# First attention of a two-layer encoder: the sample queries' scores, maxima and exponentials take later places in three queues

## The chip, the cores and the metric

The kernel runs on one core of a Trainium2 chip. The metric is the device time of one execution in microseconds (us). TensorE (PE) multiplies matrices, VectorE (DVE) and ScalarE (ACT) work on tiles, GpSimd (POOL) does small elementwise work, SyncE (SP) issues the DMAs. Each engine takes its own instructions in the order in which the program lists them; a wait on a semaphore holds everything behind it on that engine.

## The reference

Two request groups share the weights: a prompt of 1024 tokens with no history, and a sample of 32 tokens with 512 cached ones. There are two layers; the first is differential attention with a block-causal mask, the second stick-breaking attention. Each branch has a SiLU gate, an output projection and a second gated addition. Only the first attention is touched.

```python
def _diff_attn(h, pos, w_in, ...):
    q, k, v, g = jnp.split(h @ w_in, 4, axis=-1)
    q = _rope(q...); k = _rope(k...)
    k_all, v_all = with the cached keys and values ahead
    lam = exp(sum(lq1 * lk1)) - exp(sum(lq2 * lk2)) + lam_init
    def block(qb, qpb):                       # 128 queries
        s = einsum('bqhcd,bkhcd->bhcqk', qb, kf) * A_DH ** -0.5
        mask = k_chunk[None, :] <= (qpb // CHUNK)[:, None]
        pr = softmax(where(mask, s, NEG_INF), axis=-1)
        w = pr[:, :, 0] - lam * pr[:, :, 1]
        return einsum('bhqk,bkhe->bqhe', w, vf)
    o = _rmsnorm(sweep(block), sub_g) * (1.0 - lam_init)
    return (o * silu(g)) @ w_out, k, v
```

There are 8 heads of two components (c = 0, 1) with 64 features each; keys and queries of a head fill 128 partitions together.

## The kernel before

`diff_layer` computes the first attention, one group for each of the 8 heads. Groups 1 to 7 run in a loop (`more` is true: they also prepare the next group), the eighth stands behind it (`more` is false). In a group the work is laid out by hand in stages j = 2 to 13, and each engine's program has its own list of what it does in stage j. There are nine units u of queries: 0 to 7 are 128 prompt queries against (u + 1) * 128 keys, and unit 8 (`NT`) is the 32 sample queries against 544 keys. In the text of the prediction, scores(8) is the scores of unit 8, and so on.

A unit goes through these steps, each in the queue of one engine:

- PE `scores(u)` (stage u + 2): matmuls of queries and keys into the PSUM tile `la_sc`, each product in three passes of high and low parts. From u = 4 on it waits until both `probs(u - 1)` have read the tile.
- DVE `maxima(u)` (stage u + 3): the mask, and for both components the row maximum (L606) and its negative (L608).
- ACT `probs(u, c)` (stage u + 3): exponentials (L418) into `la_p`, with their sums.
- DVE `combine(u)` (stage u + 4): reciprocals and the difference of the two components (L615 to L621); the result is called weights(u) in the prediction.
- PE `turn_weights(u, g)` (L807): transposes of these weights, group g = 0 in stage u + 4, g = 1 in stage u + 5.
- ACT `move(u, g)` (L436, L432): the transposed weights to SBUF.
- PE `values(c)` (L831): weights by values, for queries of units 0 to 3 (c = 0, stage 8), of units 4 to 7 (c = 1, stage 12), and of the sample (c = 2, stage 13).

Between these stand other pieces of work. Stages 9, 10 and 11 hold the gate's three pieces (0, 1, 2): PE `gate_project` in an early part (5 of 8 rows of weights) and a late part, ACT `gate_raw`, then for the piece of the stage before DVE `gate_clamp`, ACT `gate_log`, DVE `gate_soft`, ACT `gate_sigmoid`, and POOL's product. In the same stages ACT (`split_w`, L390, tile `la_w_high`) and DVE (`split_w`, L569, tile `la_w_low`) split the next group's weight rows 0 to 2, 3 to 5 and 6 to 7 into high and low parts. From stage 12 on PE projects the first two token tiles of the next group (`project(ahead, ...)`, L105): the early part uses rows 0 to 4, the late part rows 5 to 7, and for the first tile it waits for each row's low part.

The order in stages 10 and 11 of the kernel before is:

| stage | PE | DVE | ACT |
|---|---|---|---|
| 10 | gate 1 early, turn_weights(5,1), gate 1 late, scores(8), turn_weights(6,0) | maxima(7), gate_clamp(0), combine(6), gate_soft(0), split rows 3 to 5 | probs(7), move(5,1), gate_log(0), gate_raw(1), gate_sigmoid(0), move(6,0), split rows 3 to 5 |
| 11 | gate 2 early, turn_weights(6,1), gate 2 late, turn_weights(7,0) | maxima(8), gate_clamp(1), combine(7), gate_soft(1), split rows 6, 7 | probs(8), move(6,1), gate_log(1), gate_raw(2), gate_sigmoid(1), move(7,0), split rows 6, 7 |

Stage 12 is: on PE the early part of the first tile ahead, turn_weights(7,1), its late part, turn_weights(8,0), values(1); on DVE gate_clamp(2), combine(8), gate_soft(2), finish(0); on ACT move(7,1), gate_log(2), gate_sigmoid(2), move(8,0).

Of the kernel before, what the change touches and what calls it, by code (L numbers as in the profile page):

```python
# [32 lines left out]
NT = SEQ // P  # L33
# [191 lines left out]
def diff_layer(nc, top, name, h, w_in, k_past, v_past, k_out, v_out, o_dram, w_out, ident, neg_lam, gain, cos, sin, stage):  # L225
# [14 lines left out]
    def groups_of(u):  # L240

        if u == NT:
            return [(0, PB + 1)]
        return [(k, min(4, u + 1 - k)) for k in range(0, u + 1, 4)]
# [4 lines left out]
    with ExitStack() as ctx:  # L249
# [19 lines left out]
                     scores=9, neg_max=18, probs=18, weights=9, w_turned=13, moved=13, pv=3, squared=3, var=3, log=3,  # L269
# [113 lines left out]
        def _(act):  # L383
# [19 lines left out]
            def turned_high(at, t):  # L403
                act.wait_ge(S["turned"], at.nth("turned", t + 1))
                act.activation(qk[0][:, :, tile_cols(t)], turned_bank(t), ACT.Copy).then_inc(S["turned_high"], 1)

            def body(r, more):
# [14 lines left out]
                def move(u, g):  # L422
                    q0, n, nk = UNITS[u]
                    if u < 4:
                        act.wait_ge(S["pv"], at.before("pv"))
                    elif u == 4:
                        act.wait_ge(S["pv"], at.nth("pv", 1))
                    act.wait_ge(S["w_turned"], at.nth("w_turned", moves_before(u) + g + 1))
                    k0, nb = groups_of(u)[g]
                    bank = pj[:, 2, 0:nb * n].rearrange("p (b n) -> p b n", n=n)  # L430
                    if u == NT:
                        act.activation(wt_sample[:, 0:PB, :], bank[:, 0:PB, :], ACT.Copy)  # L432
                        ins = act.activation(wt_sample[0:DEC, PB, :], bank[0:DEC, PB, :], ACT.Copy)
                    else:
                        off = q0 % QC
                        ins = act.activation(wt[:, k0:k0 + nb, off:off + n], bank, ACT.Copy)  # L436
                    ins.then_inc(S["moved"], 1)
# [35 lines left out]
                def next_tokens(t):  # L473

                    act.wait_ge(S["pv"], at.nth("pv", 2))
                    act.wait_ge(S["tok_stored"], at.all("tok_stored"))
                    tokens(ahead, t)

                for j in range(2, LAST + 1):
                    if more and j == 13:  # L480
                        next_tokens(0)
                    if j == 9:
                        square(0)
                    if j == LAST:
                        square(1)
                    if 0 <= j - 3 <= NT:
                        probs(j - 3, 0)
                        probs(j - 3, 1)
                    if j <= 9:
                        turned_high(at, j - 1)  # L490
                    if 0 <= j - 5 <= NT and len(groups_of(j - 5)) > 1:
                        move(j - 5, 1)
                    if j - 1 in GATE_AT:
                        gate_log(GATE_AT[j - 1])
                    if j <= 8:
                        act.wait_ge(S["pv"], at.before("pv"))
                        tokens(at, j)
                    if j in GATE_AT:
                        gate_raw(GATE_AT[j])
                    if j - 1 in GATE_AT:  # L500
                        gate_sigmoid(GATE_AT[j - 1])
                    if j == PAST_AT:
                        act.wait_ge(S["past_turned"], at.all("past_turned"))
                        act.activation(kpt[0][:, :], past_bank, ACT.Copy).then_inc(S["past_high"], 1)
                    if j == 9:
                        norm(0)
                    if 0 <= j - 4 <= NT:
                        move(j - 4, 0)
                    if more and j in WEIGHTS_AT:
                        if j == 9:  # L510
                            act.wait_ge(S["pj_tok"], at.all("pj_tok"))
                        for k in WEIGHTS_AT[j]:
                            split_w(r + 1, k)
                    if more and j == 13:
                        turned_high(ahead, 0)
                    if j == 13:
                        square(2)
                    if more and j in GATE_WEIGHTS_AT:
                        act.wait_ge(S["g_ready"], at.all("g_ready"))
                        split_gate(r + 1, GATE_WEIGHTS_AT[j])  # L520
                    if not more and j in BLOCKS_AT:
                        act.wait_ge(S["g_ready"], at.all("g_ready"))
                        for k in BLOCKS_AT[j]:
                            split_block(k)
                    if more and j == 13:
                        next_tokens(1)
# [27 lines left out]
        def _(dve):  # L554
# [37 lines left out]
            def body(r, more):  # L592
# [53 lines left out]
                                             op1=ALU.max).then_inc(S["g_soft"], 1)  # L646

                for j in range(2, LAST + 1):
                    if 0 <= j - 3 <= NT:
                        maxima(j - 3)  # L650
                    if j - 1 in GATE_AT:
                        gate_clamp(GATE_AT[j - 1])
                    if 0 <= j - 4 <= NT:
                        combine(j - 4)
                    if j <= 9:
                        turned_low(at, j - 1)
                    if j - 1 in GATE_AT:
                        gate_soft(GATE_AT[j - 1])
                    if j == PAST_AT:
                        dve.wait_ge(S["past_high"], at.all("past_high"))  # L660
                        dve.tensor_tensor(kpt[1][:, :], past_bank, kpt[0][:, :].bitcast(F32),
                                          ALU.subtract).then_inc(S["past_low"], 1)
                    if j == 9:
                        normalize(0)
                    if more and j in WEIGHTS_AT:
                        for k in WEIGHTS_AT[j]:
                            split_w(r + 1, k)
                    if j == 12:
                        finish(0)
                    if more and j == 13:  # L670
                        turned_low(ahead, 0)
                    if more and j in GATE_WEIGHTS_AT:
                        split_gate(r + 1, GATE_WEIGHTS_AT[j])
                    if not more and j in BLOCKS_AT:
                        for k in BLOCKS_AT[j]:
                            split_block(k)
# [59 lines left out]
        def _(pe):  # L736
# [26 lines left out]
            def body(r, more):  # L763
# [104 lines left out]
                for j in range(2, LAST + 1):  # L868
                    if j <= 8:
                        free_bank(j)  # L870
                        project(at, j, EARLY)
                    if j in GATE_AT:
                        gate_project(GATE_AT[j], EARLY)
                    if more and j >= 12:
                        free_bank(j - 12)
                        project(ahead, j - 12, EARLY)
                    if j <= 9:
                        turn(at, j - 1)
                    if more and j == 13:
                        turn(ahead, 0)  # L880
                    if 0 <= j - 5 <= NT and len(groups_of(j - 5)) > 1:
                        turn_weights(j - 5, 1)
                    if j == 13:
                        values(2)
                    if j <= 8:
                        project(at, j, LATE)
                    if j in GATE_AT:
                        gate_project(GATE_AT[j], LATE)
                    if more and j >= 12:
                        project(ahead, j - 12, LATE)  # L890
                    if j == PAST_AT:
                        pe.wait_ge(S["past"], at.nth("past", 32))
                        pe.wait_ge(S["turned_low"], at.nth("turned_low", PAST_AT))
                        for b in range(PB):
                            last = pe.transpose(past_bank[:, b * P:(b + 1) * P], kp[:, b, :], ident[:, :])
                        last.then_inc(S["past_turned"], 1)
                    if j == 9:
                        variance(0)
                    if 0 <= j - 2 <= NT:
                        scores(j - 2)  # L900
                    if 0 <= j - 4 <= NT:
                        turn_weights(j - 4, 0)
                    if j == 8:
                        values(0)
                    if j == 12:
                        values(1)
# [1366 lines left out]
```

## Time and profile before

| | us |
|---|---|
| three runs | 2142.21, 2143.97, 2143.99 (median 2143.97) |
| the profiled execution, its own time | 2142.42 |
| span of the profile, first to last instruction | 2140.7 |
| PE busy in it | 1922.7 (90%) |
| DVE busy | 1248.0 (58%) |
| ACT busy | 1019.1 (48%) |
| mean granted clock of TensorE | 0.954 |

The first attention lies between about 50 and 745 us of the span. The page's busy shares are averages over phases with different limits, so the stages that the change touches are read in the timelines of the engines, around 207 to 225 us (group 2). The idle time in brackets in a timeline stands ahead of the row's first instruction, with what released it. The groups are counted from 1.

### The profile page before, as it was taken

The numbers are of one execution on the slowest core, as the hardware profiler recorded it, in microseconds if no ns is written. First come the engines' busy times: TensorE is split into PE (matmuls) and PEld (weight loads), VectorE is DVE, ScalarE is ACT, GpSimd is POOL, SyncE is SP. The second block draws the span as 40 slices with busy tenths as digits, with TensorE's granted clock in tenths as the row PEclk, the third lists the DMA queues.
The fourth block names the chain that finished last, engine by engine and source line by source line (L and its number), as shares of the span: only waits on it lengthen the run. The fifth ranks groups of instructions, "written<-read, shape, count | busy, mean of one in ns | idle before, by whom it ended". The sixth has DMA issues, their size and how long they took to land. (4 is left out here: it accounts for less than half of the span.)

```text
span 2140.7 us, 35557 instructions
## 1 busy us (share of the span) xinstructions
PE 1922.7 (90%) x11420; PEld 1652.1 (77%) x11420; DVE 1248.0 (58%) x2629; ACT 1019.1 (48%) x2385; POOL 346.4 (16%) x565
## 2 busy tenths in 40 slices
PE   3999989999899699996899999999999999679996
PEld 2877878778788599995777777777777777479995
DVE  4456555564464622554376768686868686743455
ACT  5455454454554611454354646464646464532345
POOL 0111111111111000453011111020202021100341
PEclk9999999999999899997999999999999999989998
DMA  4121111111211232122010101010101011133213
GB/s 130 50 61 50 48 45 55 59 35 53 60 46 45 103 104 83 58 66 66 24 56 26 55 25 55 25 55 25 55 25 55 30 50 46 71 100 96 62 43 125
DMA packets 161891, 124.22 MB, mean 58 GB/s; under 512 B 11136, under 2 KB 152768, under 8 KB 161792
## 3 DMA queue, kind: packets, MB, share of 16 engines
q1 hardware_dynamic: 161792, 123.08, 19.1%
q8 instruction: 40, 0.66, 0.1%
q14 instruction: 59, 0.48, 0.1%
HBM read 89.53 MB, written 33.52 MB: 57 GB/s over the span
## 5 line engine op out<-in xcount | busy, mean ns | idle before, releaser
L105 PE MATMUL lb_pj<-lb_w_high,h_high 128*128 128x384 f32 (+1 forms) x576 | 209.8, 364 | 19.9 <-DVE lb_w_low L1273 10.7
L105 PE MATMUL la_pj<-la_w_high,h_high 128*128 128x384 f32 (+1 forms) x576 | 208.2, 361 | 7.0 <-DVE la_w_low L569 7.0
L105 PE MATMUL lb_pj<-lb_w_high,h_low 128*128 128x384 f32 (+1 forms) x576 | 201.1, 349 | 0.0
L105 PE MATMUL lb_pj<-lb_w_low,h_high 128*128 128x384 f32 (+1 forms) x576 | 200.4, 348 | 0.0
L105 PE MATMUL la_pj<-la_w_low,h_high 128*128 128x384 f32 (+1 forms) x576 | 195.8, 340 | 0.0
L105 PE MATMUL la_pj<-la_w_high,h_low 128*128 128x384 f32 (+1 forms) x576 | 195.1, 339 | 0.0
L1454 POOL TENSOR_TENSOR lb_o<-lb_o,lb_keep 128x512 f32<-128x512 f32 (+3 forms) x80 | 78.8, 984 | 605.2 <-ACT lb_keep L1156 605.2
L1132 ACT ACTIVATE lb_m<-lb_m 128x512 f32<-128x512 f32 (+4 forms) x200 | 98.7, 521 | 148.4 <-DVE lb_m L1294 146.4
L1307 DVE TENSOR_TENSOR lb_s<-lb_sc,lb_m 128x512 f32<-128x512 f32 (+4 forms) x200 | 110.0, 550 | 47.4 <-ACT lb_m L1137 47.3
L1294 DVE TENSOR_SCALAR lb_m<-lb_sc 128x512 f32<-128x512 f32 (+4 forms) x200 | 101.3, 546 | 61.4 <-PE lb_sc L1533 46.0
L418 ACT ACTIVATE la_p<-la_sc,la_nm 128x128 f32<-128x128 f32 (+5 forms) x144 | 106.0, 738 | 57.9 <-DVE la_nm L608 56.0
L105 PEld LDWEIGHTS lb_pj<-lb_w_high,h_high 128*128 128x128 f32 (+1 forms) x576 | 109.1, 189 | 30.3 <-issue 11.7
L105 PEld LDWEIGHTS la_pj<-la_w_high,h_high 128*128 128x128 f32 (+1 forms) x576 | 105.3, 183 | 12.7 <-issue 6.8
L105 PEld LDWEIGHTS lb_pj<-lb_w_high,h_low 128*128 128x128 f32 (+1 forms) x576 | 108.9, 189 | 5.9
L105 PEld LDWEIGHTS lb_pj<-lb_w_low,h_high 128*128 128x128 f32 (+1 forms) x576 | 108.0, 188 | 4.3
L1346 DVE TENSOR_TENSOR lb_s_low<-lb_s,lb_s_high 128x512 fp32r<-128x512 f32 (+1 forms) x192 | 107.3, 559 | 6.6
L606 DVE TENSOR_REDUCE la_mx<-la_sc 128x1 f32<-128x128 f32 (+5 forms) x144 | 107.6, 747 | 3.0 <-DVE la_sc L601 0.2
L105 PEld LDWEIGHTS la_pj<-la_w_low,h_high 128*128 128x128 f32 (+1 forms) x576 | 104.5, 181 | 4.3
L105 PEld LDWEIGHTS la_pj<-la_w_high,h_low 128*128 128x128 f32 (+1 forms) x576 | 105.1, 182 | 3.2
L1555 PE MATMUL lb_sc<-lb_s_high,lb_tri 128*128 128x512 f32 (+1 forms) x192 | 82.3, 428 | 14.0 <-DVE lb_s_low L1346 14.0
L1344 DVE CAST lb_s_high<-lb_s 128x512 fp32r<-128x512 f32 (+1 forms) x192 | 78.3, 408 | 27.6 <-DVE lb_s L1313 2.4
L1137 ACT ACTIVATE lb_m<-lb_m 128x512 f32<-128x512 f32 (+4 forms) x200 | 92.2, 506 | 0.3
(296 smaller groups left out, 5256.2 us busy)
## 6 DMA issues: line engine op xcount, KB each, us to landing
stage<-in_a_w_in SPq DMA_DIRECT2D x60, 192.0 KB, 3.1
stage<-in_b_w_in SPq DMA_DIRECT2D x60, 192.0 KB, 2.6
stage<-in_ple_w_gate SPq DMA_DIRECT2D x22, 512.0 KB, 3.9
h_low<-o_t SPq DMA_DIRECT2D x14, 528.0 KB, 6.2
mix_b_xs<-x_mid SPq DMA_DIRECT2D x8, 528.0 KB
norm_a_xt<-in_x SPq DMA_DIRECT2D x8, 512.0 KB, 3.6
stage<-in_a_w_in SPq DMA_DIRECT2D x16, 256.0 KB, 5.4
out_ak<-la_tok SPq DMA_DIRECT2D x8, 512.0 KB, 3.3
```

The costliest lines, as they stand in the source:

```text
L105: last = pe.matmul(out, x, y, start=start and n == 0, stop=stop and n == 2, **kw)
L418: act.activation(p[c][u % (3 - c)][0:n, 0:nk], scores_of(u)[:, c, :], ACT.Exp, bias=nm[0:n, u % 2, c:c + 1], accum_out=sums[0:n, u % 2, c: ...
L606: dve.reduce_max(mx[0:n, u % 2, c:c + 1], x[:, c, :], AX.X).then_inc(S["dve_link"], 1)
L1132: act.activation(x, x, ACT.Exp).then_inc(S["exp"], 1)
L1137: act.activation(x, x, ACT.Ln, bias=1.0).then_inc(S["log"], 1)
L1294: dve.tensor_scalar(x, slot, SOFT_MAX, None, ALU.min).then_inc(S["clamped"], 1)
L1307: ins = dve.tensor_tensor(sp, slot, x, ALU.max)
L1344: dve.tensor_copy(high, sp).then_inc(S["high"], 1)
L1346: dve.tensor_tensor(low, sp, high.bitcast(F32), ALU.subtract).then_inc(S["low"], 1)
L1454: pool.tensor_tensor(out, out, kept[n % 2][:, q:], ALU.mult).then_inc(S["scaled"], 1)
L1555: last = pe.matmul(slot, tri[:, :], part, **add)
```

## The change

In PE's list, `scores(8)` leaves stage 10, where it stood ahead of turn_weights(6,0), and stands in stage 11 behind the early part of gate piece 2 and ahead of turn_weights(6,1). In DVE's list, `maxima(8)` stays in stage 11 but stands behind gate_clamp(1) and combine(7) and ahead of gate_soft(1). In ACT's list, the two `probs(8, c)` stay in stage 11 but stand behind move(7,0) and ahead of the split of rows 6 and 7. Nothing is added or taken away; waits and semaphores of the moved steps are the same.

```diff
@@ ACT's list
-                    if 0 <= j - 3 <= NT:
+                    if 0 <= j - 3 < NT:
                         probs(j - 3, 0)
                         probs(j - 3, 1)
...
                     if 0 <= j - 4 <= NT:
                         move(j - 4, 0)
+                    if j - 3 == NT:
+                        probs(NT, 0)
+                        probs(NT, 1)
                     if more and j in WEIGHTS_AT:
@@ DVE's list
-                    if 0 <= j - 3 <= NT:
+                    if 0 <= j - 3 < NT:
                         maxima(j - 3)
                     if j - 1 in GATE_AT:
                         gate_clamp(GATE_AT[j - 1])
                     if 0 <= j - 4 <= NT:
                         combine(j - 4)
+                    if j - 3 == NT:
+                        maxima(NT)
                     if j <= 9:
@@ PE's list
                     if j in GATE_AT:
                         gate_project(GATE_AT[j], EARLY)
+                    if j - 3 == NT:
+                        scores(NT)
...
-                    if 0 <= j - 2 <= NT:
+                    if 0 <= j - 2 < NT:
                         scores(j - 2)
```

## Rows read from the trace of the kernel before

**Rows 1.** The page's span; the table of PE's waits, 74 to 740 us.

```profile
span 2140.7 us, 35557 instructions
...
PE la_sc L790 <- ACT la_p L418: 20.1, 8, 2.8
PE la_pj L807 <- DVE la_p L621: 16.1, 13, 3.0
```

**Rows 2.** Timeline of PE, group 2: start, duration, instruction, [idle before, releaser].

```profile
209.65 0.42 PE L790 MATMUL la_sc<-la_kpt_high,la_qk_high 64*32 64x512 f32 x2 [2.83 <-ACT la_p L418]
...
210.91 0.97 PE L807 MATMUL la_pj<-ident,la_p 128*128 128x128 f32 x4 [0.30 <-DVE la_p L621]
...
215.38 0.49 PE L807 MATMUL la_pj<-ident,la_p 128*128 128x128 f32 x3
...
219.00 0.65 PE L807 MATMUL la_pj<-ident,la_p 128*128 128x128 f32 x4 [1.69 <-DVE la_p L621]
...
224.19 0.46 PE L807 MATMUL la_pj<-ident,la_p 32*128 32x32 f32 x5
```

**Rows 3.** Timeline of DVE, group 2.

```profile
214.37 0.70 DVE L606 TENSOR_REDUCE la_mx<-la_sc 32x1 f32<-32x544 f32 x1
...
216.09 0.34 DVE L639 TENSOR_SCALAR la_gtmp<-la_gate 128x352 f32<-128x352 f32 x1
...
217.58 1.28 DVE L621 SCALAR_TENSOR_TENSOR la_p<-la_p,la_sums 128x1024 f32<-128x1024 f32 x1
218.78 0.52 DVE L645 SCALAR_TENSOR_TENSOR la_gtmp<-la_gate,la_gtmp 128x352 f32<-128x352 f32 x1
220.76 1.03 DVE L569 TENSOR_TENSOR la_w_low<-stage,la_w_high 128x384 fp32r<-128x384 f32 x2 [1.46 <-ACT la_w_high L390]
...
222.91 0.78 DVE L621 SCALAR_TENSOR_TENSOR la_p<-la_p,la_sums 32x544 f32<-32x544 f32 x1
```

**Rows 4.** Timeline of ACT, group 2.

```profile
215.29 0.71 ACT L418 ACTIVATE la_p<-la_sc,la_nm 32x544 f32<-32x544 f32 x1 [1.54 <-DVE la_nm L608]
...
216.80 0.46 ACT L436 ACTIVATE la_wt<-la_pj 128x384 f32<-128x384 f32 x1
...
219.34 0.50 ACT L455 ACTIVATE la_gtmp<-la_gtmp 128x352 f32<-128x352 f32 x1 [0.81 <-DVE la_gtmp L645]
219.74 0.58 ACT L436 ACTIVATE la_wt<-la_pj 128x512 f32<-128x512 f32 x1
220.22 0.93 ACT L390 ACTIVATE la_w_high<-stage 128x384 fp32r<-128x384 f32 x2
```

**Rows 5.** Stretches of group 2: engines' busy us, PEclk the granted clock, DMA share, GB/s.

```profile
206.90:209.60 2.70, 0.00 (x0) 0.00 (x0) 2.59 (x7) 2.51 (x5) 0.00 (x0) 1.00 0.30 100
211.50:214.80 3.30, 3.30 (x14) 3.30 (x13) 1.84 (x4) 2.11 (x5) 0.94 (x1) 0.54 0.02 7
```

**Rows 6.** Timeline of PE: groups 1, 3 (three rows), 5 and 6.

```profile
134.45 0.65 PE L807 MATMUL la_pj<-ident,la_p 128*128 128x128 f32 x4 [2.04 <-DVE la_p L621]
...
295.47 0.65 PE L807 MATMUL la_pj<-ident,la_p 128*128 128x128 f32 x4 [0.31 <-DVE la_p L621]
...
303.29 1.11 PE L807 MATMUL la_pj<-ident,la_p 128*128 128x128 f32 x4 [3.00 <-DVE la_p L621]
...
310.06 0.46 PE L807 MATMUL la_pj<-ident,la_p 32*128 32x32 f32 x5
...
474.14 0.65 PE L807 MATMUL la_pj<-ident,la_p 128*128 128x128 f32 x4 [1.29 <-DVE la_p L621]
...
559.15 1.03 PE L807 MATMUL la_pj<-ident,la_p 128*128 128x128 f32 x4 [2.70 <-DVE la_p L621]
```

**Rows 7.** Timeline of PE, the last group.

```profile
718.90 0.66 PE L807 MATMUL la_pj<-ident,la_p 128*128 128x128 f32 x4
...
721.80 0.49 PE L807 MATMUL la_pj<-ident,la_p 128*128 128x128 f32 x3
...
727.07 0.43 PE L807 MATMUL la_pj<-ident,la_p 32*128 32x32 f32 x5 [1.00 <-DVE la_p L621]
```

## The prediction

> **What bounds the kernel now.** Read first the page's span and the table of waits of the first attention: TensorE (PE) waits there for ScalarE's exponentials of block 7 (`la_p`, 20.1 us in eight waits, at most 2.8) and for VectorE's finished weights (`la_p` L621, 16.1 us) [rows 1]. The loop over head groups takes 84.56 us from the transposes of block 6's weights in group 2 to those in group 3 [rows 2, 6], and eight groups run. Then read PE's timeline of group 2 [rows 2]. In stage j=10 PE is queued at scores(8), the sample's, which wait for probs(7): 2.83 us idle. They start at 209.65; 0.30 us of the time to 210.91 is a second wait, for weights(6), so the scores cost PE 1.26 - 0.30 = 0.96 us. The transposes of weights(6), called T here, start at 210.91, those of weights(7) at 219.00 after a wait of 1.69, those of weights(8) at 224.19, T + 13.28. Last, read VectorE (DVE) and ScalarE (ACT) beside it [rows 3, 4]: they are the cause of the waits, and DVE is nearly full from T on. From weights(8) to the next T it is 295.47 - 224.19 = 71.28 us, a stretch in which PE is queued without waiting for this chain, so I take a shift of weights(8) to pass on in full.
>
> **The change, part by part.**
>
> 1. scores(8) leave j=10. The 2.83 us wait is gone by name, but the next item in PE's queue is T, which waits for weights(6), released at about 210.8. In group 2 the 0.30 us says so [rows 2]. So T stays at 210.91, and PE idles 2.83 + 0.96 + 0.30 = 4.1 us in one piece. Gain: 0. Bound below: where the clock was low ahead of T, T was late by about 0.3 us, and that is won (one or two groups).
>
> 2. scores(8) return after the early part of gate piece 2: +0.96 us on PE between T and weights(7). They start at about 215.4 and are done at 216.4 [rows 2]. Their wait for probs(7) is long over. Arrival at weights(7): 219.00 - 1.69 + 0.96 = 218.3.
>
> 3. maxima(8) move behind combine(7) on DVE. They take 216.09 - 214.37 = 1.72 us [rows 3], so weights(7) are ready 1.72 us earlier, at 217.3. PE gets there at 218.3, before 219.00: 0.7 us won at this point. In group 3, where PE waited 3.00 us, the full 1.72 are won [rows 6]. Queued behind the moved maxima is gate_soft(1); the sum clamp, combine, maxima is the same in either order, so it starts at 218.78 as before, provided scores(8) are done by 217.06. They are, with 0.7 us to spare.
>
> 4. probs(8) move on ACT behind move(7,0), and this is the dear part. Before they ran from 215.29 to 216.80 (1.51 us), in time in which ACT had nothing else to do: it idled 1.54 us ahead of them and 0.81 us later for gate_soft(1) [rows 4]. Now ACT comes to move(6,1) at 216.8 as before (its transposes end about then), waits for gate_soft(1) as before, runs gate_sigmoid(1) at 219.34 and move(7,0) at 219.74, and at 220.22, where it began the splits of weight rows 6 and 7 for the next group, it runs probs(8). The splits begin at 220.22 + 1.51 = 221.73. Queued behind them are all of j=12's work on ACT and, through w_high, DVE.
>
> 5. What is late next. DVE's low parts of these two rows started at 220.76 and now start at 222.27 [rows 3]. PE's late part of the projection ahead needs them: it would be at them at about 221.5 and waits until 222.8 and 223.3, ending near 223.9, still before 224.19. Behind the low parts on DVE stand clamp(2) and combine(8): its last instruction ran from 222.91 for 0.78 us, to 223.69, and now ends at 225.20. Transposes of weights(8): 225.20 + 0.14 = 225.34 against 224.19, **+1.15 us**. Behind them on PE stand values(1), which nothing else covers, and the rest of the group. That they were not bound by weights(8) before is 0.36 us of slack; the other 1.15 of the 1.51 comes through.
>
> 6. Other groups. Five of the seven groups that split weights look like group 2: waits for weights(7) of 1.29 to 2.04 us [rows 6]. I take +1.1 for four of these and +0.8 for the one whose T is won 0.3 earlier. The other two (3 and 6, waits 3.00 and 2.70) had the low clock after that wait: there PE reached weights(8) late, at T + 14.59 in group 3, while by the chain above they are ready at T + 14.2. They give back 0.4 and 0.7. Sum of seven: 4 x 1.12 + 0.8 - 0.4 - 0.7 = +4.2.
>
> 7. The last group splits no weights, so weights(8) come earlier, and there DVE and ACT were close behind PE already: waits of 1.00 us at weights(8) [rows 7]. Now the early part ends at 721.80, scores(8) at 722.8, after combine(7) is done (about 722.1), so maxima(8) wait: to 724.5; gate_soft(1) 0.5, gate_sigmoid(1) 0.45, move(7,0) 0.5, probs(8) 1.5, combine(8) 1.8 (clamp to last instruction as in [rows 3], less the clamp) and 0.14 put the transposes at 729.4 to 729.6, against 727.07. **+2.5 us**. What follows is written in series (values(1), square, variance, norm, finish, the next phase), so I pass it on in full; no row here proves that.
>
> 8. The clock. While PE idles 2.7 us the granted clock is still 1.00 and right after it is 0.54, the lower of the two levels (1.2 GHz) for most of the stretch 211.5 to 214.8 [rows 5]. A piece of 3.3 us at the lower level costs PE half of that, about 1.7 us. With 4.1 us of idle time ahead of T it will fall in all groups, at times earlier and for longer. Mostly this is hidden: PE now has about 2.3 us of idle time between T and weights(8), at the late rows and at weights(8). It costs when it makes scores(8) late for maxima(8) (0.6 us, say two groups) or when the new idle time makes the clock fall again, so that it is values(1) that run slow (1.7 us; no more than one group taken, since the waits of 1.3 to 2.0 us did not do that and those of 2.7 and 3.0 did [rows 6]). Bound: -1.7 (one low piece fewer) to +8 us; I take +1.4, since the waits that are nearest in length mostly did not lower it.
>
> Sum: +4.2 + 2.5 + 1.4 = **+8.1 us**. The profiled run took 2142.42 us with a span of 2140.7, so 2150.5; the other three of before run from 2142.21 to 2143.99, median 2143.97, so against that it is +6.5. Faster or slower is by over 0.2% here, about what a measurement of this kernel can tell from no change, 4.3 us.
>
> The Trainium skill, TensorE: Matmul & The Clock Gate, section "Why this matters for your kernels", says to leave no long gap between bursts of matmuls, since idling puts the array back to half rate. This case's trace agrees as far as the fall after the gap of group 2 goes (1.00, then 0.54). By that rule alone the longer gap is a loss in itself in every group, which is rival A; by my sum it is mostly covered.
>
> **Rivals.**
>
> A. The clock decides. The joined gap ahead of T keeps the lower level for twice as long, so scores(8) and maxima(8) are late in most groups (0.6 to 1.2 us each), and the idle time ahead of weights(8) brings it down again in half of them (1.7 us each). That is +6 to +10 on top of steps 1 to 7: about 2156. For it: two waits in [rows 6] had this after them. Against: five did not. Chance 0.15. The rule of the Trainium skill named above points this way.
>
> B. PE stays the bound to weights(8), no change: if the two split rows and combine(8) come out 1 us earlier than worked out (ACT's move(6,1) or the gate steps shorter), the five groups give 0, two give back 1 to 2 each as in group 3, the last costs 1 to 2: about 2142.5, in 2140 to 2146. Against: probs(8) and the splits stand on one in-order engine with its next wait above them. Chance 0.13.
>
> C. Faster: the earlier weights(7) of step 3 come through. The place is the transposes of weights(7), the price 0.7 us in five groups and 1.7 in two: 2142.4 - 5 x 0.7 - 2 x 1.7 = 2135.5. It decides if PE reaches weights(8) without waiting, that is if the low rows and combine(8) end no later than before. For it: PE is the engine that is queued in most of the loop. Against: steps 4 and 5. Chance 0.08.
>
> That the change takes away the whole gap ahead of T, as it says of the queries ahead, would be 7 x 2.83 = 20 us, 2122. The 0.30 us wait on weights(6) behind the scores speaks against it [rows 2], and combine(6) is not moved. Chance 0.02.
>
> D. My forecast, slower, +8: it decides from the point at which probs(8) ahead of the splits take more than the 0.36 us of slack. Chance 0.62.
>
> **Numbers.** 2150.5, its own range 2146.5 to 2154.5. With A and part of B, 8 in 10: 2142 to 2157; clock pieces of the rest of the program (one piece is 1.7 us) are in it. Slower by over 0.2%: D nearly whole and A, 0.73; within: B and the low end of D, 0.17; faster: 0.10.
>
> **What will show it.** PE's wait at L790 for `la_p` L418 gone, and a wait of about 4 us at L807 for weights(6) in its place; the wait for weights(7) gone or under 0.5; new waits of PE for the low weight rows at L105 and of about 1.4 us for weights(8) at L807; ACT's L390 pair starting 1.5 us later after T; weights(8) at T + 14.2 to 14.5; the last group 2 to 2.5 us longer. It is wrong if T comes earlier than in the kernel before relative to the maxima of block 7, if weights(8) start by T + 13.4, or if the stretch from there to the next T is not 71.3 us.

## The result and the profile after

| | before | after |
|---|---|---|
| median of all runs, us | 2143.89 (8 runs, 2138.65 to 2146.35) | 2156.42 (8 runs, 2151.53 to 2160.24) |
| profiled execution, us | 2142.42 | 2159.87 |
| its span, us | 2140.7 | 2158.1 |

The ratio is 1.006, with a 95% interval of 1.0049 to 1.0071: the kernel became slower, by 12.5 us in the medians. The forecast was 2150.5, +6.5 against the median that was known then, so the change is nearly twice as large as forecast. The median lies outside the forecast's own range (2146.5 to 2154.5) and just inside the wider one (2142 to 2157). The direction and the path were right, the size was not. One execution each of two experiments below (4604 us in e3, 2907 us in e6) stands far above all others and is left out of the ratios.

The page's span and the table of PE's waits in the first attention (74 to 760 us; total, times, longest), to be read against [rows 1]:

```profile
span 2158.1 us, 35557 instructions
...
PE la_pj L812 <- DVE la_p L624: 41.1, 16, 4.1
PE la_pj L105 <- DVE la_w_low L572: 1.4, 2, 0.7
PE la_pj L812 <- ACT la_wt L436: 1.3, 1, 1.3
```

L812 is the transposes of weights (L807 before), L624 combine's last instruction (L621 before). The wait for the exponentials of block 7, 20.1 us, is gone. The wait for finished weights grew from 16.1 to 41.1 us.

Timeline of PE in group 2, against [rows 2]:

```profile
215.46 1.11 PE L812 MATMUL la_pj<-ident,la_p 128*128 128x128 f32 x4 [4.10 <-DVE la_p L624]
...
219.72 0.41 PE L795 MATMUL la_sc<-la_kpt_high,la_qk_high 64*32 64x512 f32 x2
...
220.61 0.55 PE L812 MATMUL la_pj<-ident,la_p 128*128 128x128 f32 x3
...
222.45 0.60 PE L812 MATMUL la_pj<-ident,la_p 128*128 128x128 f32 x4
...
227.30 0.44 PE L105 MATMUL la_pj<-la_w_high,h_high 128*128 128x384 f32 x1 [0.68 <-DVE la_w_low L572]
...
229.85 0.43 PE L812 MATMUL la_pj<-ident,la_p 32*128 32x32 f32 x5 [1.23 <-DVE la_p L624]
```

The same stretch of DVE and of ACT, against [rows 3, 4]:

```profile
221.74 0.71 DVE L609 TENSOR_REDUCE la_mx<-la_sc 32x1 f32<-32x544 f32 x1
...
223.36 0.50 DVE L648 SCALAR_TENSOR_TENSOR la_gtmp<-la_gate,la_gtmp 128x352 f32<-128x352 f32 x1
226.69 1.03 DVE L572 TENSOR_TENSOR la_w_low<-stage,la_w_high 128x384 fp32r<-128x384 f32 x2 [2.83 <-ACT la_w_high L390]
...
228.83 0.77 DVE L624 SCALAR_TENSOR_TENSOR la_p<-la_p,la_sums 32x544 f32<-32x544 f32 x1
```

```profile
221.20 0.49 ACT L436 ACTIVATE la_wt<-la_pj 128x384 f32<-128x384 f32 x1 [2.76 <-PE la_pj L812]
...
224.30 0.58 ACT L436 ACTIVATE la_wt<-la_pj 128x512 f32<-128x512 f32 x1
224.78 0.69 ACT L418 ACTIVATE la_p<-la_sc,la_nm 32x544 f32<-32x544 f32 x1
...
226.15 0.92 ACT L390 ACTIVATE la_w_high<-stage 128x384 fp32r<-128x384 f32 x2
```

Read the three together. The 2.83 us of waiting, the 0.96 us of scores and 0.30 us became one wait of 4.10 us ahead of T. Weights(7) follow at T + 7.0 without a wait (T + 8.1 before). Then ACT runs probs(8) for 1.37 us ahead of the splits, DVE waits 2.83 us for them (1.46 before), its combine(8) ends late, and weights(8) start at T + 14.39 instead of T + 13.28, after a new wait of 1.23 us.

All groups, from the same kind of rows (us):

| group | 1 | 2 | 3 | 4 | 5 | 6 | 7 | last |
|---|---|---|---|---|---|---|---|---|
| T to weights(8), before | 13.42 | 13.28 | 14.59 | 13.05 | 13.43 | 15.02 | 13.05 | 8.17 |
| T to weights(8), after | 14.00 | 14.39 | 15.08 | 14.67 | 15.15 | 14.72 | 14.40 | 10.72 |
| weights(8) to next T, before | 71.26 | 71.28 | 71.26 | 71.55 | 71.57 | 71.27 | 68.64 | |
| weights(8) to next T, after | 72.94 | 71.24 | 71.24 | 72.91 | 71.24 | 72.93 | 68.62 | |

The spans differ by 17.4 us, and this is all of it: 6.6 from T to weights(8) in the seven looped groups, 2.55 in the last group, 4.3 behind weights(8), 2.3 ahead of the first T (128.52 instead of 126.23) and 1.7 behind the last weights(8).

Stretches of the kernel after (columns as in [rows 5]; PEclk, the granted clock, is the third number from the end): right after T in group 2, inside values(1) in group 4, from the start of values(1) in the last group, and in the first group far ahead of any moved instruction.

```profile
215.50:218.30 2.80, 2.80 (x11) 2.80 (x12) 0.94 (x3) 2.27 (x6) 0.94 (x1) 0.51 0.00 0
...
402.80:406.20 3.40, 3.40 (x5) 1.29 (x5) 0.91 (x2) 0.76 (x4) 0.93 (x1) 0.53 0.16 47
...
743.00:750.00 7.00, 7.00 (x17) 3.19 (x16) 3.15 (x4) 2.67 (x5) 0.93 (x1) 0.76 0.84 342
...
60.00:72.00 12.00, 8.71 (x36) 8.39 (x35) 1.12 (x2) 2.00 (x6) 2.12 (x8) 0.72 0.55 155
```

In the second of them the clock is at 1.2 GHz for most of a stretch of values(1), behind the new wait for weights(8); this is what makes 72.9 of 71.2 in groups 1, 4 and 6. The third shows the same in the last group, behind a wait of 2.50 us for weights(8); the kernel before had 1.00 there (727 to 734 us). A mean of 0.76 over 7 us is 3.4 us at half the speed, which costs about 1.7 us, and that is the 1.7 behind the last weights(8). The fourth is 0.72 where the kernel before had 1.00 in the same stretch. No instruction of that stretch was changed. The first T lay between 124.58 and 126.75 us in five experiments below (e1, e2, e3, e5, e6) that change nothing ahead of stage 10 either, so about 2 us of the profile's 17.4 are what one execution differs from another, and the medians (12.5) are the better measure.

### The profile page after: what moved, and what is told of

Same layout as the page of the kernel before. It is cut to its first block and busy times, and to the rows that moved or that the text cites. A ratio compares the mean times of both kernels' runs of the same rounds, so it can differ in the third digit from the quotient of the medians.

```text
span 2158.1 us, 35557 instructions
## 1 busy us (share of the span) xinstructions
PE 1932.9 (90%) x11420; PEld 1656.3 (77%) x11420; DVE 1247.4 (58%) x2629; ACT 1018.8 (47%) x2385; POOL 346.5 (16%) x565
## 5 line engine op out<-in xcount | busy, mean ns | idle before, releaser
L1139 ACT ACTIVATE lb_m<-lb_m 128x512 f32<-128x512 f32 (+4 forms) x200 | 98.7, 521 | 150.0 <-DVE lb_m L1301 148.1
L105 PEld LDWEIGHTS la_pj<-la_w_high,h_high 128*128 128x128 f32 (+1 forms) x576 | 105.5, 183 | 15.9 <-issue 6.8
L812 PE MATMUL la_pj<-ident,la_p 128*128 128x128 f32 (+2 forms) x328 | 57.4, 289 | 42.4 <-DVE la_p L624 41.1
```

The costliest lines, as they stand in the source:

```text
L105: last = pe.matmul(out, x, y, start=start and n == 0, stop=stop and n == 2, **kw)
L812: last = pe.transpose(bank[0:rows, b, :], p[0][u % 3][0:n, k:k + rows], ident[0:n, 0:n])
L1139: act.activation(x, x, ACT.Exp).then_inc(S["exp"], 1)
```

## The experiments

The theory: from T on, DVE and ACT are queued, and weights(8) come when ACT's list from probs(7) to the splits and DVE's combine(8) are through; the moved probs(8) lengthen it. The rivals: PE's idle time ahead of T is worth its length; the clock decides; the moved scores are the loss. The ratios are to the kernel before, run beside each experiment on the same chip (its medians there were 2143.4 to 2144.0), with 95% intervals.

**e1, only the scores moved.** PE's part of the change alone:

```diff
                     if j in GATE_AT:
                         gate_project(GATE_AT[j], EARLY)
+                    if j - 3 == NT:
+                        scores(NT)
...
-                    if 0 <= j - 2 <= NT:
+                    if 0 <= j - 2 < NT:
                         scores(j - 2)
```

> Only scores(8) move to the place behind the early part of gate piece 2; maxima(8) and probs(8) stay at the head of stage 11. Theory (the chain on DVE and ACT from T to weights(8) sets the end): maxima(8) find their scores not ready and wait at the head of DVE's stage 11 for 0.5 to 3 us, by how long the clock is low, with combine(7) and on ACT the splits queued behind; weights(8) at T + 14.5 to 16, PE's wait ahead of T 4.1 us as in the changed kernel; 2152 to 2162 us. Rival (PE's idle time ahead of T is what can be won): not slower than the kernel before.

Measured: 2172.38 us, ratio 1.013 (1.0116 to 1.0145), outside the range on the slow side. DVE and PE in group 2 (T is 212.62):

```profile
218.16 0.71 DVE L606 TENSOR_REDUCE la_mx<-la_sc 32x1 f32<-32x544 f32 x1 [2.22 <-PE la_sc L790]
```

```profile
229.56 0.46 PE L807 MATMUL la_pj<-ident,la_p 32*128 32x32 f32 x5
```

DVE waits 2.2 us for the late scores with combine(7) queued behind, and weights(8) are at T + 16.74 to T + 17.64. The mechanism is the expected one and its length was under-sized: PE reaches the scores under the low clock (granted 0.68 from 212.6 to 218 us). So moving maxima(8) was needed once scores(8) moved; the change's own parts repair 16 us of what its first part costs.

**e2, the scores back.** The changed kernel with scores(8) in stage 10 again, the reverse of that diff.

> The changed kernel with scores(8) back in stage 10 ahead of turn_weights(6,0); maxima(8) and probs(8) stay late. Theory: T is unmoved, PE waits 2.8 us for probs(7) and 0.3 us for weights(6) again, and weights(8) are still at T + 14.2 to 14.4, since the splits wait for probs(8): the loss of step 4 without PE's part, 2148 to 2152 us. What is left to the measured 2156 is then the longer gap and the lower clock behind it. If PE's move is itself the loss: 2144.

Measured: 2154.36 us, ratio 1.0054 (1.0038 to 1.0069). PE in group 2:

```profile
213.35 1.11 PE L812 MATMUL la_pj<-ident,la_p 128*128 128x128 f32 x4 [0.28 <-DVE la_p L624]
...
227.74 0.43 PE L812 MATMUL la_pj<-ident,la_p 32*128 32x32 f32 x5 [1.22 <-DVE la_p L624]
```

Weights(8) are at T + 14.39 in six of seven groups. T did not gain from the scores' going, and 10.4 of the 12.5 us of loss are there with PE's list untouched: most of it is in the lists of ACT and DVE. The median is 2.4 us above the range; two groups had the low clock behind weights(8).

**e3, probs(8) behind the splits.**

```diff
-                    if j - 3 == NT:
-                        probs(NT, 0)
-                        probs(NT, 1)
                     if more and j in WEIGHTS_AT:
...
                         for k in WEIGHTS_AT[j]:
                             split_w(r + 1, k)
+                    if j - 3 == NT:
+                        probs(NT, 0)
+                        probs(NT, 1)
```

> The changed kernel with probs(8) on ACT behind the split of rows 6 and 7 and not ahead of it. Theory: the low rows come 1.5 us earlier and PE no longer waits for them, weights(8) follow probs(8) directly, 221.15 + 1.51 + 1.7 + 0.14 on group 2's clock, at T + 13.6 and not T + 14.4: 5 to 6 us less than the changed kernel, 2150 to 2152. If the order of probs(8) and splits is not what costs: 2156, the wait at weights(8) unchanged.

Measured: 2147.28 us, ratio 1.0016 (1.0007 to 1.0025): 9 us less than the changed kernel, by two ACT instructions' place. ACT and PE in group 2 (T is 210.92):

```profile
220.24 0.93 ACT L390 ACTIVATE la_w_high<-stage 128x384 fp32r<-128x384 f32 x2
221.07 0.69 ACT L418 ACTIVATE la_p<-la_sc,la_nm 32x544 f32<-32x544 f32 x1
```

```profile
224.54 0.43 PE L812 MATMUL la_pj<-ident,la_p 32*128 32x32 f32 x5 [1.13 <-DVE la_p L624]
```

Weights(8) are at T + 13.62 here, as expected (T + 13.22 to 14.10 in the seven groups), PE has no wait for low rows left, and the stretches from weights(8) to the next T are at their least (71.2, and 68.6 in group 7): the clock did not fall in values(1) in any group, though PE waited 0.70 to 1.35 us ahead of weights(8). The changed kernel lost 5.0 us there, which can be why e3 did better than expected; in the last group of e3 the clock did fall (0.75 behind a wait of 2.50 us).

**e4, combine(6) early.**

```diff
-                    if 0 <= j - 4 <= NT:
+                    if 0 <= j - 4 <= NT and j != 10:
                         combine(j - 4)
...
                     if j == 9:
+                        combine(6)
                         normalize(0)
```

> The changed kernel with combine(6) on DVE in stage 9, ahead of normalize(0), in time in which DVE idles. T then hangs on ACT's move(5,1), which frees the bank of the transposes at about 209.8 on group 2's clock and not on weights(6) at 210.8: wait ahead of T 3.0 us instead of 4.1, released by ACT L436. Theory: ACT's chain from probs(7) on is unmoved, so weights(8) come at most 0.3 us a group earlier against maxima(7), and the time is 2153 to 2157. Rival (the idle time ahead of T is worth its length): 1.1 us in eight groups, 2147 or less.

Measured: 2155.36 us, ratio 1.0047 (1.0034 to 1.006). PE in group 2:

```profile
212.73 1.11 PE L813 MATMUL la_pj<-ident,la_p 128*128 128x128 f32 x4 [3.02 <-ACT la_wt L436]
...
227.81 0.43 PE L813 MATMUL la_pj<-ident,la_p 32*128 32x32 f32 x5 [1.23 <-DVE la_p L624]
```

T comes 1.1 us earlier and is now released by ACT's move(5,1); weights(8) are at T + 15.08 in seven groups. Of the 1.08 us that T won, 0.69 are given back against group 2 of the changed kernel. The other 0.39 is the delay by the low clock that is gone, not the earlier T: weights(8) come 17.94 us after the start of probs(7), as in group 1 of the changed kernel (17.94) and as in e6 below with the late T and the clock high (17.95).

**e7, the gap closed.** e4, and ACT's `move(5, 1)` ahead of `probs(7, 0)`, in 2.4 us in which ACT waited for the maxima of block 7.

> The changed kernel with combine(6) in DVE's stage 9 and ACT's move(5,1) ahead of probs(7): nothing holds the transposes of weights(6) any more, and PE reaches T without a wait, 3.9 us earlier. Theory: ACT's chain from probs(7) over move(6,0), splits, gate steps and probs(8) is unmoved, so the 3.9 us come back as waits at turn_weights(6,1), weights(7) and weights(8), at about T + 18: 2148 to 2157 us. Rival (PE's gap ahead of T is worth its length): 4.1 us in seven groups, about 2127.

Measured: 2149.65 us, ratio 1.0027 (1.0017 to 1.0038). PE in group 2:

```profile
208.33 0.60 PE L815 MATMUL la_pj<-ident,la_p 128*128 128x128 f32 x4
...
218.43 0.65 PE L815 MATMUL la_pj<-ident,la_p 128*128 128x128 f32 x4 [2.71 <-DVE la_p L626]
...
226.32 0.43 PE L815 MATMUL la_pj<-ident,la_p 32*128 32x32 f32 x5 [1.22 <-DVE la_p L626]
```

T has no wait at all, and weights(8) come at T + 17.98 in place of T + 14.4. The 4.1 us moved to later waits: 1.4 at turn_weights(6,1), 2.7 at weights(7), 1.1 at a low row and 1.2 at weights(8). This falsifies the rival that the idle time ahead of T is worth its length: 4.1 us in each of seven groups removed, 6.8 us won. Weights(8) come 17.66 us after the start of probs(7), only 0.3 us earlier than in e4 and e6, and no stretch behind weights(8) of the seven groups was above its least value; the three long ones had cost the changed kernel 5.0 us.

**e5, one ACT instruction more.** Behind the two `probs(NT, c)` of the changed kernel:

```diff
+                        act.activation(sq[0:DEC, 0:PAST], sq[0:DEC, 0:PAST], ACT.Square)
```

> The changed kernel with one more ScalarE instruction of 32 x 512 elements behind probs(8) and ahead of the split of rows 6 and 7; it rewrites a scratch tile that is dead there. By the rows of the changed kernel such an instruction holds the engine for 0.5 us. Theory (what ACT does between move(7,0) and the splits is on the path): weights(8) at T + 14.9 instead of T + 14.4, +0.5 us in seven groups and none in the last, which has no splits, if combine(8) follows probs(8) there: +3 to +4 us, near 2160. If ACT has room there: 2156.

ACT in group 2:

```profile
222.97 0.61 ACT L512 ACTIVATE la_sq<-la_sq 32x512 f32<-32x512 f32 x1
223.49 0.92 ACT L390 ACTIVATE la_w_high<-stage 128x384 fp32r<-128x384 f32 x2
```

In the profile the dose is as expected: it holds ACT for 0.52 us, and the seven T to weights(8) sum to 105.5 us instead of 102.4; the least of them go from 14.00 to 14.51. The median, 2164.61 us (ratio 1.0103, 1.0088 to 1.0117), is 8 us above the changed kernel, twice the expected 3 to 4. The profiled execution took 2157.79 us, the lowest of four (up to 2169.78), so its trace doesn't show where the others spent the rest; that stays open.

**e6, PE filled ahead of T.** In the changed kernel, ahead of `turn_weights(6, 0)`:

```diff
+                    if j == 10:
+                        pe.wait_ge(S["normed"], at.nth("normed", 1))
+                        for _ in range(14):
+                            pe.matmul(acc[:, :], h[0][:, 0, 0:P], h[0][:, 0, 0:512], start=True, stop=True)
```

> The changed kernel with 14 matmuls of 512 columns into a free bank in PE's gap ahead of T, about 3 us of work that nobody reads; T must not move. Theory: the clock stays at 2.4 GHz (granted 1.0) from T on, so weights(8) are at T + 14.1 in all groups and not at T + 14.0 to 15.1; what the low clock ahead of and behind T costs is this difference, 0.5 us a group and 4 to 5 us in all. The wait ahead of weights(8) stays, and PE idles longer ahead of it, so the low clock inside values(1) (1.7 us in three groups) may stay too: 2148 to 2154 us. If the time is 2156 or more, the clock's part of the loss is not set by the gap.

Measured: 2155.19 us, ratio 1.0055 (1.0042 to 1.0068). A row of PE in group 4 (T is 385.21), and the stretches T to weights(8) and values(1) of group 2:

```profile
399.22 0.43 PE L812 MATMUL la_pj<-ident,la_p 32*128 32x32 f32 x5 [1.23 <-DVE la_p L624]
```

```profile
213.00:227.00 14.00, 11.43 (x75) 9.86 (x75) 9.41 (x22) 8.94 (x21) 1.89 (x2) 1.00 0.05 14
227.10:232.00 4.90, 4.90 (x12) 2.48 (x13) 1.61 (x3) 1.25 (x4) 0.93 (x1) 0.65 0.22 66
```

With the gap filled the clock stays at 1.00 from T to weights(8), which come at T + 14.01 or 14.02 in all seven groups. So the low clock behind the gap costs 14.6 - 14.0 = 0.6 us a group, 4.3 in seven. But the median is only 1.2 us below the changed kernel's, which the intervals don't tell from nothing, and 1.2 us above the expected range. The trace shows two reasons. The clock fell in values(1) all the same (0.65 in the last row): weights(8) to T took 74.49 and 72.88 us in groups 1 and 2, 4.9 us lost where the changed kernel lost 5.0. And in the last group, where the gap ahead of T is only 1.36 us, the filler holds T itself:

```profile
722.16 3.36 PE L911 MATMUL la_acc<-h_high 128*128 128x512 f32 x14
725.36 0.60 PE L812 MATMUL la_pj<-ident,la_p 128*128 128x128 f32 x4
```

There T comes 1.7 us late (70.33 us behind the weights(8) of group 7 instead of 68.62). So T did not stay in place there, and by the trace 1.7 us of what the filled gap won went to the filler itself.

**e8, reordered.** PE as in the changed kernel; combine(6) early and `move(5, 1)` early as in e7; `probs(8)` back at the head of ACT's stage 11; on DVE:

```diff
                     if j - 1 in GATE_AT:
                         gate_soft(GATE_AT[j - 1])
+                    if j == 10:
+                        combine(7)
+                        maxima(8)
...
+                    if j == 11:
+                        combine(8)
```

> A version for less time. PE as in the changed kernel (scores(8) behind the early part of gate piece 2). DVE: combine(6) in stage 9, combine(7) and maxima(8) in stage 10 behind gate_soft(0) and ahead of the low parts of rows 3 to 5, combine(8) in stage 11 ahead of gate_soft(1). ACT: move(5,1) ahead of probs(7), probs(8) at the head of stage 11 as in the kernel before. Theory: DVE does these steps while ACT is busy with the gate and the splits, the waits of ACT for maxima(8) (1.5 us) and gate_soft(1) (0.8 us) shrink, and weights(8) come 2 to 4 us earlier a group against maxima(7): 2112 to 2128 us. If ACT and DVE have no room: 2140 or more.

Measured: 2141.24 us, ratio 0.9979 (0.9967 to 0.9991). It is the first one below the kernel before, and far above the range I gave. DVE and PE in group 2:

```profile
209.86 0.52 DVE L647 SCALAR_TENSOR_TENSOR la_gtmp<-la_gate,la_gtmp 128x352 f32<-128x352 f32 x1 [1.90 <-ACT la_gtmp L450]
```

```profile
211.45 0.55 PE L816 MATMUL la_pj<-ident,la_p 128*128 128x128 f32 x3 [1.45 <-ACT la_wt L436]
...
216.25 0.66 PE L816 MATMUL la_pj<-ident,la_p 128*128 128x128 f32 x4 [2.80 <-ACT la_wt L436]
...
223.02 0.46 PE L816 MATMUL la_pj<-ident,la_p 32*128 32x32 f32 x5
```

DVE stood 1.9 us at gate_soft(0) for gate_log(0), about the last 1.0 us of it with the exponentials of block 7 ready (208.9), and PE waited for ACT's moves, which stood behind gate steps. The expectation had overlooked that gate steps nobody needs soon hold both lists.

**e9, the gate's steps later.** e8, with these lists of ACT for stages 10 to 12, and gate_soft(0) behind maxima(8), gate_soft(1) behind the low rows 6 and 7 on DVE:

```diff
+                    if j == 10:
+                        move(5, 1)
+                        probs(7, 0)
+                        probs(7, 1)
+                        move(6, 0)
+                        ...split rows 3 to 5
+                        gate_log(0)
+                        gate_raw(1)
+                    if j == 11:
+                        move(6, 1)
+                        probs(8, 0)
+                        probs(8, 1)
+                        gate_sigmoid(0)
+                        gate_raw(2)
+                        move(7, 0)
+                        ...split rows 6 and 7
+                        gate_log(1)
+                    if j == 12:
+                        move(7, 1)
+                        gate_sigmoid(1)
+                        move(8, 0)
+                        gate_log(2)
+                        gate_sigmoid(2)
```

> Run e8 showed weights(8) only 0.6 us a group earlier against maxima(7) than in the kernel before: DVE waited 1.9 us for gate_log(0) ahead of combine(7), and ACT came to move(6,0) only behind the gate steps, with PE waiting for it. Here the gate's steps stand behind: ACT runs probs(7), move(6,0), rows 3 to 5, gate_log(0), gate_raw(1); then move(6,1), probs(8), gate_sigmoid(0), gate_raw(2), move(7,0), rows 6 and 7, gate_log(1); then move(7,1), gate_sigmoid(1), move(8,0), gate_log(2), gate_sigmoid(2). DVE runs maxima(7), gate_clamp(0), combine(7), maxima(8), gate_soft(0), rows 3 to 5; then gate_clamp(1), combine(8), rows 6 and 7, gate_soft(1). Theory (the queues of ACT and DVE between probs(7) and weights(8) are the bound, and the gate's steps can wait for the time of values(1)): T without a wait, weights(7) at about T + 6 to 7, weights(8) at T + 11 to 13 instead of T + 16 to 18 in e8, 4 to 5 us a group: 2100 to 2120 us. If the loads of rows 6 and 7, which wait for the low parts of rows 2 and 3, come late: weights(8) at T + 14, 2125.

Measured: 2105.09 us, ratio 0.9818 (0.9805 to 0.9831). Table of PE's waits in it (74 to 745 us), and PE in group 2:

```profile
PE la_pj L105 <- DVE la_w_low L600: 7.2, 7, 1.0
PE la_pj L847 <- ACT la_wt L436: 5.2, 9, 1.6
```

```profile
201.85 0.60 PE L847 MATMUL la_pj<-ident,la_p 128*128 128x128 f32 x4
...
208.13 0.66 PE L847 MATMUL la_pj<-ident,la_p 128*128 128x128 f32 x4 [0.41 <-ACT la_wt L436]
...
214.63 0.46 PE L847 MATMUL la_pj<-ident,la_p 32*128 32x32 f32 x5
```

T is reached without a wait, 0.41 us are left at weights(7) and none at weights(8), at T + 12.8. Together with the 66.98 to 67.01 us from there to the next T a group takes 79.8 us (84.56 before). All of these steps do the kernel's own work, so this is a full version, 38 us faster than the kernel before and 51 us faster than the changed one. It differs from e8 in several places at once (the gate's steps, the splits ahead of them, two steps of DVE), and what each of them gives is not separated.

**e10, e9 with the scores back.** The reverse of e1's diff on e9.

> Run e9 with PE's scores(8) back in stage 10 ahead of turn_weights(6,0), as in the kernel before. Theory: the change's PE part does nothing while DVE and ACT hold T (e2), but is worth its length once they don't: here PE stands at scores(8) for probs(7) for about 2.8 us, T comes 3.7 us later than in e9, and ACT's move(6,0) and splits with it, by 1.7 us or more; weights(8) 1.5 to 3 us later a group than in e9, 2115 to 2128 us. If the place of scores(8) is indifferent: 2105.

Measured: 2123.4 us, ratio 0.9905 (0.9889 to 0.9922). Its largest wait of PE (74 to 740 us):

```profile
PE la_sc L830 <- ACT la_p L418: 21.1, 8, 2.8
```

The old wait is back in full, and now it costs nearly what it shows: 2123.4 - 2105.1 = 18.3 us. Weights(8) come 14.7 to 14.95 us after the start of probs(7) in six of the seven groups, instead of 12.5 in e9. The granted clock is lower too (0.96 instead of 0.99 from 74 to 740 us), and its part in this is not separated. So the new place of scores(8) is good by itself, but only when nothing else holds T and the maxima.

## Why the prediction was right, and where its sizes were off

- **Step 1, T unmoved:** right. T starts 3.9 us after probs(7) in group 2 before and after. The wait ahead of T is 4.10 us in all seven looped groups (4.1 forecast), and e2 has T at the same place with the scores back.
- **Steps 2 and 3:** right. The scores cost PE 220.61 - 219.72 = 0.89 us (0.96). No wait for weights(7) is left. The waits for the low weight rows that step 5 expects came in two groups only (0.7 us each).
- **Steps 4 and 5, the term that carried the forecast:** right, +1.11 us in group 2 (+1.15), with the splits at T + 10.69 instead of T + 9.31, a shift of 1.38 us. e3 and e5 show it from both sides: probs(8) behind the splits take 0.77 us from T + 14.39, half a microsecond more in front adds 0.51 where the clock was as high (group 1, 14.00 to 14.51). That the size in group 2 came out so well is partly luck: 0.38 us of its T + 14.39 are the low clock, which this step left out (T + 14.01 in e6), and probs(8) took 1.37 us and not 1.51.
- **Step 6:** the sum of the seven groups was +4.2, measured +6.6. Two errors partly cancel. With the clock high, as in e6, the sum is 98.1 - 95.8 = +2.3; the low clock behind the longer gap, counted apart in step 8, adds 4.3. Group 6 gave back 0.3 us (0.7 forecast), group 3 none: T to weights(8) rose there from 14.59 to 15.08. In group 3 before, part of the 14.59 was a low clock after the long wait for weights(7); after, the low clock had its place ahead of and behind T instead.
- **The path of the low clock ahead of weights(8)** was named only in part in step 8. Scores(8) were late for maxima(8) in two groups, as it says, by 0.29 us (group 3) and 0.36 us (group 5) instead of 0.6:

```profile
481.73 0.71 DVE L609 TENSOR_REDUCE la_mx<-la_sc 32x1 f32<-32x544 f32 x1 [0.36 <-PE la_sc L795]
```

  Two more places were left out. T's own transposes take 1.11 us instead of 0.65 in six of the seven groups, so move(6,0) and the splits behind it start late; DVE waits 1.86 us for them and not 1.46, and combine(7) behind them is 0.4 us late. And ACT's move(6,1), whose transposes stand behind the scores on PE, is late:

```profile
482.20 0.49 ACT L436 ACTIVATE la_wt<-la_pj 128x384 f32<-128x384 f32 x1 [4.23 <-PE la_pj L812]
```

  This is T + 7.2 (T is 474.99) against T + 5.7 in group 2. Gate_log(1) follows it, and DVE waits 0.2 us for that at gate_soft(1) in groups 3 to 6; step 4 had passed move(6,1) over with "its transposes end about then". All three together are the 0.6 us a group that e6 takes away.
- **Step 7, the last group:** right, +2.55 (+2.5). DVE waits for probs(8) there:

```profile
740.90 0.15 DVE L618 RECIPROCAL la_sums<-la_sums 32x2 f32<-32x2 f32 x1 [2.09 <-ACT la_p L418]
```

- **Step 8, the clock:** this is the term that was mis-sized. I took +1.4 us for it. In the profile T to weights(8), the stretches behind it, the last group and its values(1) together are 6.6 + 4.3 + 2.55 + 1.7 = 15.1 us, where steps 6 and 7 had 6.7 without the clock: that leaves 8.4 us for it. I allowed one group's values(1) to run at 1.2 GHz; it was three of the seven (+4.3 us in the sum) and the last group as well (+1.7), and the falsifier I gave, a stretch behind weights(8) other than 71.3, came in for the three. I had taken the length of a wait as what decides, from waits of 1.3 to 2.0 us that had no effect. It doesn't: PE waited 1.21 to 1.23 us ahead of weights(8) in all seven groups, and the clock fell in groups 1, 4 and 6 and not in the others. What picks the groups is open. Rival A had this as its mechanism, with +6 to +10 us for it, and lay, with 2156, nearest to the median; that the forecast's wider range holds the median is owed to rival A. What its mechanism has too large is how often scores(8) are late (two groups, not most). The direction did not hang on it: with T to weights(8) as in e6 and no other low clock, 2.3 + 2.55 = 4.9 us of the change would be left by my estimate, and they come from the lists of ACT and DVE, as e2 and e3 show. What page and forecast made of the clock differs less than it seemed: by TensorE: Matmul & The Clock Gate of the Trainium skill (section "Why this matters for your kernels") a gap between bursts is what loses the full rate. e6 agrees as to the stretch behind the gap (1.00 all through with the gap filled), but there the clock fell in values(1) all the same and the median moved by 1.2 us only, which the rule alone would not have told.
- **Rivals B and C** fell: weights(8) do wait in every group; weights(7) came 1.1 us earlier after T in group 2 and weights(8) still later; and e4 and e7 show what an earlier T is worth with ACT's list as it is.

## What to carry to other kernels

A long wait of PE is not a price until the next item in its queue is known to be free: here the wait hid a second one, and behind both stood a list of ACT. When a step is moved into a later place, look there for who is queued behind it, and for the idle time that it leaves: ACT was idle around the old place, and at the new one the splits stood behind it. What pays is to order each engine's list by when its results are needed; here the gate's steps stood ahead of moves and exponentials that PE waited for. The order of e8 alone won 0.2%; with the gate's steps put behind as well (e9) it was 1.8%.

## What the runs showed of the hardware

The granted clock is not told by the length of the wait ahead of it. Behind waits of 1.21 to 1.23 us ahead of weights(8) it fell to 1.2 GHz in values(1) in three of seven groups of the changed kernel, in two of e2 and of e6, in one of e4 and in three of e5, and in none of e7 (1.02 to 1.22 us). Behind waits of 1.3 to 2.0 us in the kernel before it stayed at 1.00 in all five groups [rows 6]. In the last group, behind a wait of 2.50 us, it fell in every version that had this wait. In e6, where the gap ahead of T was filled and the clock stayed at 1.00 up to weights(8), it fell in values(1) all the same. A term for it needs a range of some 1.7 us for every group that has a wait at all (3.2 in one group of e6). And one execution can differ from another by some 2 us before it reaches changed work: the first T lay at 128.52 us in the changed kernel, with a granted clock of 0.72 between 60 and 72 us, and at 126.23 with 1.00 in the kernel before.
